# The order of the query tiles within a head pair in the last attention stage of a two-block transformer kernel

## The reference, cut to what matters

```
s_sel = jnp.einsum('bqhgd,bhqkd->bhgqk', qc, kg).astype(f32) * scale
p_sel = masked_softmax(s_sel, (key_pos <= t[:, None])[:, :, None])
o_sel = jnp.einsum('bhgqk,bhqkd->bqhgd', p_sel.astype(vg.dtype), vg)
...
s_win = jnp.einsum('bqhgd,bkhd->bhgqk', qc, kwc).astype(f32) * scale
p_win = masked_softmax(s_win, wmask)
...
o = g[..., 0:1] * o_cmp + g[..., 1:2] * unchunk(o_sel) + g[..., 2:3] * unchunk(o_win)
```

## Time and profile before

| | |
|---|---|
| median of 3 runs | 2942.43 us (2941.71 to 2944.08) |
| the profiled execution's own time | 2946.5 us |
| its span | 2944.6 us |
| instructions in the profile | 43108 |
| busy: TensorE, weight load, VectorE, ScalarE | 96%, 79%, 47%, 33% |
| chain that ended last, by engine | TensorE 90%, VectorE 6%, ScalarE 2% |
| the stage of the 32 units | about 2199.9 to 2303.0 us of the span |

### The profile page before, as it was taken

One profiled execution on the slowest core, in us unless ns is written; L12 is line 12 of the kernel. 1 busy time (PEld: TensorE's weight loads), 2 busy tenths in 40 slices (PEclk: granted clock), 3 DMA queues, 4 the chain that ended last, 5 costly groups with the idle time before them and its releaser, 6 DMA issues.

```text
span 2944.6 us, 43108 instructions
## 1 busy us (share of the span) xinstructions
PE 2826.3 (96%) x18438; PEld 2313.4 (79%) x18438; DVE 1388.8 (47%) x2453; ACT 969.7 (33%) x1561; POOL 62.8 (2%) x53
## 2 busy tenths in 40 slices
PE   7999999999999998999999999999997999999999
PEld 5876578888888887876788888887774788888887
DVE  3454553433233334326756637458477534443333
ACT  2144552422112224115635323332145322332222
POOL 2000000100000000000001002000000000000000
PEclk9989999999999999999999999999999999999999
DMA  6232101122332230110011332311220132322322
GB/s 261 87 99 73 41 13 46 58 101 104 116 124 101 103 113 29 62 60 22 1 58 61 105 108 86 115 44 58 86 83 22 58 100 93 94 79 86 108 95 85
DMA packets 67790, 238.53 MB, mean 81 GB/s; under 512 B 7440, under 2 KB 10640, under 8 KB 66960
## 3 DMA queue, kind: packets, MB, share of 16 engines
q1 hardware_dynamic: 67312, 234.20, 23.8%
q10 hardware_dynamic: 288, 1.57, 0.1%
HBM read 233.64 MB, written 2.10 MB: 80 GB/s over the span
## 4 chain that ended last, share of the span: by engine, by line
PE 90%; DVE 6%; ACT 2%; issue 1%; DMA 1%; SPq 0%; DVEq 0%; ACTq 0%
PE PSA L658 87%; PE PSA L964 2%; PE PSA L1244 1%; DVE WS L2206 1%; DMA Y<-in_early 1%; DVE stat L2989 1%; ACT Y L2070 1%; PE PSA L1554 0%; DVE HS L2376 0%; ACT Y L2077 0%; ACT WS L1644 0%; DVE PSA L2988 0%; ACT HS L1731 0%; DVE X L2314 0%; DVE X L2348 0%
## 5 line engine op out<-in xcount | busy, mean ns | idle before, releaser
L658 PE MATMUL PSA<-HS,WS 128*128 128x512 f32 (+1 forms) x6672 | 1354.8, 363 | 23.4 <-DVE HS L2376 12.8
L658 PEld LDWEIGHTS PSA<-HS,WS 128*128 128x128 f32 x6672 | 1127.5, 190 | 237.8 <-issue 34.7
L2206 DVE TENSOR_TENSOR WS<-W,WS 128x1024 fp32r<-128x1024 f32 (+2 forms) x318 | 364.1, 1147 | 608.0 <-ACT WS L1644 606.9
L1644 ACT ACTIVATE WS<-W 128x1024 fp32r<-128x1024 f32 (+2 forms) x318 | 313.8, 989 | 795.5 <-PE PSA L658 424.9
L658 PE MATMUL PSA<-YS,WS 128*128 128x512 f32 (+1 forms) x2232 | 471.1, 372 | 3.5 <-DVE YS L3021 3.5
L658 PEld LDWEIGHTS PSA<-YS,WS 128*128 128x128 f32 x2232 | 393.0, 189 | 79.4 <-DVE YS L3021 3.9
L658 PE MATMUL PSA<-Y 128*64 128x128 f32 (+8 forms) x2368 | 284.1, 341 | 18.3 <-ACT Y L1792 6.1
L658 PEld LDWEIGHTS PSA<-Y 128*64 128x64 f32 (+3 forms) x2368 | 174.1, 153 | 97.9 <-issue 70.3
L1628 ACT ACTIVATE Y<-PSA 128x512 f32<-128x512 f32 (+5 forms) x77 | 53.3, 699 | 250.7 <-PE PSA L658 250.7
L658 PE MATMUL PSA<-HS,YS 128*128 128x512 f32 (+1 forms) x696 | 127.9, 341 | 4.5 <-issue 4.1
L658 PEld LDWEIGHTS PSA<-HS,YS 128*128 128x128 f32 x696 | 107.6, 191 | 21.5 <-issue 7.3
(11 more groups left out here) (332 smaller groups left out, 2297.3 us busy)
## 6 DMA issues: line engine op xcount, KB each, us to landing
W<-in_weights SPq DMA_DIRECT2D x396, 512.0 KB, 3.5
Y<-in_early SPq DMA_DIRECT2D x4, 2048.0 KB, 19.8
W<-in_weights SPq DMA_DIRECT2D x24, 256.0 KB, 2.6
X<-in_x SPq DMA_DIRECT2D x4, 768.0 KB, 21.1
W<-in_weights SPq DMA_DIRECT2D x24, 128.0 KB, 2.1
Y<-in_ssm ACTq DMA_DIRECT2D x1, 1024.0 KB, 6.9
out<-X SPq DMA_DIRECT2D x1, 1024.0 KB, 4.6
C<-in_consts SPq DMA_DIRECT2D x1, 948.5 KB, 33.3
```

Of the source, the lines that this page charges most:

```text
L658: return pe.matmul(out, lhsT, rhs, start=first, stop=last)
L1644: act.activation(split_home(n)[:, 0, 0:f], W[:, c % W_RING, 0:f], ACT.Copy)\
L2206: tt(home[:, 1, 0:f], W[:, c % W_RING, 0:f], home[:, 0, 0:f].bitcast(F32), ALU.subtract)\
```

## The change

The query tiles of each head pair are taken in the order 0, 3, 1, 2 in place of 0, 1, 2, 3. The mark that a head pair's output is complete, and VectorE's reading of it, move from tile 3 to tile 2, now the last.

```diff
-        NSA_UNITS = [("nsa", p, i, b) for p in range(NSA_H // 2) for i in range(4) for b in range(2)]
+        NSA_UNITS = [("nsa", p, i, b) for p in range(NSA_H // 2) for i in (0, 3, 1, 2) for b in range(2)]
...
-                if i == 3 and b:
+                if i == 2 and b:
                     ins.then_inc(psum_filled[slot(key)], 1)
...
-                if n >= 4 and NSA_UNITS[n - 4][2:] == (3, 1):
+                if n >= 4 and NSA_UNITS[n - 4][2:] == (2, 1):
```

## The result

| | before | changed |
|---|---|---|
| median of 21 runs each | 2941.70 us | 2946.63 us |
| lowest and highest | 2940.41, 2949.01 us | 2943.14, 2953.68 us |
| ratio of the changed kernel to the one before | | 1.0015, 95% interval 1.0009 to 1.0021 |

The changed kernel is slower by 0.15% by the ratio, and by 4.9 us between the two medians. That is inside the 0.2% that was named as no change, but clear of noise, and 0.6 us above the range's upper end of 2946.0. The forecast was 0.7 us.

The account below looks back on a forecast made before the run. Prediction: TensorE bounds the kernel, a loop of waits between TensorE, VectorE and ScalarE the changed stage. Terms +0.3 + 0.1 + 0.6 - 0.3 = +0.7 us on the 2942.43 us median gave 2943.1 us; range 2940.6 to 2946.0.

Parts of the forecast that it names:

- What bounds the stage: Changed stage, about 103 us: a loop of waits between TensorE, VectorE and ScalarE; each microsecond there is one of the kernel.
- Same work, other order: the loop sums to 22.23 us: Two-step loop over a head pair: the same sum, 22.23 us, before and after, where the loop binds; cost 0.
- VectorE's lateness: Second round of a head pair, order of before: VectorE came about 0.74 us after TensorE's scores were ready.
- The round that VectorE binds: 6.50 us, late by 1.3: Boundary between head pairs: VectorE's round grows from 5.17 to 6.50 us, late 1.3 instead of 0.74; +0.6 us.
- The first head pair, the second and the tail (+0.3, +0.1, -0.3): Sum's terms outside the third pair: +0.3 us first pair, +0.1 second, -0.3 last pair with the stage's end.
- The walk: Loop followed start by start, each the latest of what it waits for; before's stage ended 0.5 us early against the trace.
- the clock falls in each head pair: Rival: longer gaps at the VectorE-bound round halve TensorE's clock in the last three pairs; 18 us slower, 2961 us; chance 0.02.
- The second, one stretch more or less: Rival: one half-clock stretch more or less, behind step 5 or later in the kernel; 2941.4 to 2944.8 us; chance 0.22.
- 17 gaps: TensorE's idle gaps in the later stage, order of before: at most 1.7 us, 80 us at full clock, no fall.
- "Within 0.2%": Whole kernel: the time changes by no more than 0.2% (5.9 us), taken as no change; chance 0.95.

Follow-up runs that it names:

- the filled version: Changed kernel plus four and seven throwaway matmuls in TensorE's two idle stretches of each later head pair: ratio 1.0001 to the kernel before, median 2943.17 us.
- the first filling: Changed kernel plus four throwaway matmuls in the shorter idle only, the 2.05 us ahead of the wide unit left idle: ratio 1.0015 to the kernel before, 2947.02 us.
- the half of the added VectorE work: Order of before with one of the two reading-out instructions repeated at three head-pair boundaries, 0.7 us each: ratio 1.0010, 2945.80 against 2941.47 us.
- reading out later: Changed kernel with VectorE's reading out three steps later for the first three head pairs: ratio 0.9999 to the kernel before, 2941.90 against 2942.86 us.
- the doubled reading out: Order of before with the reading out done twice at three head-pair boundaries, 1.3 us more VectorE work: ratio 1.0029, 2948.74 us.

## Why the prediction was wrong

*What bounds the stage.* Right. The two profiled stages differ by 4.7 us where the medians differ by 4.9, and the TensorE work behind it starts with its end.

*Same work, other order: the loop sums to 22.23 us.* Right, and better than I could tell from before: with VectorE's lateness and the clock falls taken out, the second and third head pair take 22.3 to 22.5 us in three kernels of two orders, and the third 22.4 us in the order of before.

*The round that VectorE binds: 6.50 us, late by 1.3.* Right. From 2250.40 (mask of unit 18) to 2256.90 (unit 20) it is 6.50 us in the changed kernel. With the clock kept up the third head pair takes 23.5 us against 23.0, the +0.6 of the sum.

*The first head pair, the second and the tail (+0.3, +0.1, -0.3).* The second and the tail were right with the clock up (23.8 and 30.1 us against the forecast's 23.7 and 29.9). The +0.3 for the first was not borne out. Its piece depends on how much half clock there is: 25.9 us in one profile of the changed kernel and 26.9 in the other, 25.0 in the four other runs whose program is the same up to there, and 26.2, 26.2, 26.2 and 27.3 in the four profiles that have the order of before.

*"The walk gives 4.4 us idle at step 5 and at most 2.0 us later ... so I price no change."* **This is the step that failed.** The idle times were right (4.33 and 2.05 us in the trace). The price was wrong. I read the two rows as ends, no fall at 1.7 and a fall at 5.04 us, and put 2.0 on the side of the nearer one, as if single stretches decided. The trace of before had a row between them, at the head of this very stage. TensorE idled 1.96 us up to 2200.27 and 0.81 us up to 2201.71, was busy 1.02 of 3.4 us, and then stood at half clock for 6.8 us:

```profile
2198.70:2202.10 3.40, 1.02 (x8) 0.72 (x8) 2.77 (x10) 2.82 (x10) 0.00 (x0) 1.00 0.00 0
2202.10:2208.90 6.80, 5.99 (x26) 2.77 (x23) 4.61 (x15) 3.43 (x14) 0.00 (x0) 0.50 0.00 0
```

The prediction says of that stretch that it began where TensorE had been idle, and did not ask for how long; two idle stretches close together is also how the new boundary looks. In the trace the clock fell in each of the three later head pairs, and the longer loop that results is 1.0, 1.2 and 2.3 us over the filled version: 4.5 us, where the stage's loss beyond the forecast 0.7 is 4.0. The later experiments say that not even the length of one stretch is the right reading: the clock fell with 1.3 us, and stayed up with 2.05 and 2.75. Why it falls at one boundary and not at another like it stays open.

*The rivals.* The first named the mechanism and the place ("the clock falls in each head pair") and mispriced it: it had TensorE at half clock through the whole of each pair, 18 us, where it was a stretch of 3.4 to 6.8 us, 0.9 to 2.4 us each. It was given 0.02. The second, one stretch more or less, had the price of a stretch right, but took it as a single accident, and not as one for each boundary. With three such stretches at the second rival's own 0.8 to 1.7 us in the sum, the forecast would have been 0.7 + 2.4 to 0.7 + 5.1, that is +3.1 to +5.8 us. The page of the Trainium skill that spoke against the change ("TensorE: Matmul & The Clock Gate", section "A second HAM failure mode: psum-queue depth-cycling", right behind the one on HAM oscillation; HAM is its name for what sets TensorE's clock) was the better guide: it tells of a kernel whose clock swings because TensorE idles briefly and often between groups of matmuls. The changed kernel agrees, with 1.31 and 2.05 us around 1.7 us of work, and three runs here show that gaps as long don't always do it: the first filling, the half of the added VectorE work in two head pairs, and all of it in one. I had held 17 gaps without a fall against it. The boundary stood out among them already:

```profile
2257.50:2260.90 3.40, 1.89 (x16) 0.92 (x14) 3.26 (x9) 1.52 (x8) 0.00 (x0) 1.00 0.02 5
```

This is the trace of before, TensorE busy 1.89 of 3.4 us and the clock at 1.00. The same place in the changed kernel, just ahead of the fall:

```profile
2254.60:2258.00 3.40, 1.35 (x13) 0.78 (x10) 3.30 (x8) 1.72 (x5) 0.00 (x0) 0.97 0.00 0
```

The 1.3 us more of VectorE's work made the place thinner, and that could be worked out beforehand: the walk had the times of both gaps. It would have been a reason to give the fall a larger chance, not to count on it, since the first filling stayed at 1.00 with the same 1.35 us.

*The chances and the range.* "Within 0.2%" was right. The range was too low by 0.6 us; a fall entered it at most once, as +1.7. Its ends and those of the second rival can't be added up from the terms named: 1.2 us off 2943.1 is 2941.9 and not 2941.4, and from 2942.43 the terms give 2940.1 to 2945.3 and not 2940.6 to 2946.0. The measured median lies outside either.

## What to carry to other kernels

In a loop where every piece's duration hangs on one unit, the order of the units doesn't change the loop's sum; it changes who is late at the seams and what the tail ends on. Worked out from the rows, these came out within 0.2 us in the later head pairs of the changed order and missed by 0.5 us a head pair where VectorE work was added. TensorE's clock is a term of that sum wherever its work thins out, even where its longest wait hardly grows. Look in the trace at hand for every stretch at half clock, see what stood ahead of each, and let a fall at each repetition stand as a rival with a fair chance. A run with a few throwaway matmuls in TensorE's idle time tells how much of a loss is the clock, if it is read in the pieces of the stage and not in the time of the whole kernel alone. Leave them out where the end of the stage waits for TensorE.

## What the runs showed of the hardware

- The clock fell once in each of the three later head pairs in both profiles of the changed order, behind idle stretches of 1.31 and 2.05 us. It also fell behind 1.32 and 0.72 us (reading out later). It stayed at 1.00 behind 2.05 us with TensorE busy 1.35 of 3.4 us (shorter idle filled, three times) and behind 2.75 us with 0.65 of 3.4 us busy (the doubled reading out, third head pair). Neither the longest idle nor how thin the work is decides by itself; what does is left open.
- A stretch at half clock lasted 3.4 or 6.8 us in the stage. At the head pairs of the changed order it cost 0.9 to 1.2 us or 2.3 to 2.4 us, against the filled version. In the order of before with added VectorE work a stretch of 3.4 us cost 0.3 us or less, by an estimate from the neighbouring head pairs.
- Stretches at half clock differ between executions of one program: in the changed kernel's two profiles the one behind step 5 lasted 3.4 and 6.8 us. The times of the 21 runs of the changed kernel go with their mean granted clock: 2943.14 us at 0.984, 2953.68 us at 0.979. Two profiles of unchanged code ahead of the stage differ by 5.7 us, with a lower clock in the slower.
- Throwaway matmuls held the clock at 1.00 in the head pairs, and the filled pieces took about the forecast's time. They cost 1.2 us where they stood in the serial end of the stage.
